# Expert layer: each slot tile split after its last block, all four multiplied as split pairs into banks 4 to 7, and h added bank by bank

## What is computed

```python
def hier_moe(xn, w_group, b_group, w_expert, b_expert, w_gate, w_up, w_down):
    ...
    cw = jnp.einsum('tk,tke->te', comb, jax.nn.one_hot(expert_id, N_EXPERTS, ...))
    hid = jax.nn.silu(jnp.einsum('td,edf->tef', xt, w_gate)) * jnp.einsum('td,edf->tef', xt, w_up)
    y = jnp.einsum('tef,efd->td', hid * cw[:, :, None], w_down)
    return y.reshape(b, s, d)
...
        h = h + hier_moe(rms_norm_2(h, ln_ffn[i]), ...)
        gate = jax.nn.sigmoid(rms_norm_2(h, ln_ple[i]) @ ple_w_gate[i])
        h = h + (gate * (p[i] @ ple_w_proj[i])).astype(h.dtype)
```

## Time and profile before

| | us |
|---|---|
| median of 3 executions | 1210.54 |
| lowest, highest | 1205.42, 1211.98 |
| the profiled execution, its own time | 1211.84 |
| its span, first to last instruction | 1210.1 |
| TensorE busy | 1090.7 (90%) |
| VectorE busy | 763.8 (63%) |
| ScalarE busy | 720.8 (60%) |
| mean granted TensorE clock | 0.946 of full speed |

### The profile page before, as it was taken

The page is one execution under the profiler, slowest core; times in us unless marked ns, Lnnn a source line. Parts: engine busy times, 40 slices in busy tenths (PEclk is TensorE's granted clock), DMA queues, the critical chain, the costliest instruction groups (busy, mean ns, idle before and its releaser), DMA issues.

```text
span 1210.1 us, 17394 instructions
## 1 busy us (share of the span) xinstructions
PE 1090.7 (90%) x6140; PEld 905.5 (75%) x6140; DVE 763.8 (63%) x1331; ACT 720.8 (60%) x1228; POOL 72.2 (6%) x111
## 2 busy tenths in 40 slices
PE   5968889999999997899979999978979969999988
PEld 4857677999998785797667777747868767787756
DVE  4536664666665665456567778765755467778864
ACT  4435664444443544385649888835656549988834
POOL 9000600000000012000100000000000100000000
PEclk9987699999999999899989999998989979999998
DMA  9784003665654545002507999853601607999830
GB/s 291 182 206 151 1 10 126 212 191 177 191 187 147 178 139 186 2 2 87 209 25 255 327 322 329 308 169 112 191 15 36 261 3 258 338 328 335 305 138 35
DMA packets 105083, 210.79 MB, mean 174 GB/s; under 512 B 7992, under 2 KB 49816, under 8 KB 104752
## 3 DMA queue, kind: packets, MB, share of 16 engines
q1 hardware_dynamic: 101984, 204.04, 49.4%
q0 software_dynamic: 2736, 4.80, 2.2%
q10 hardware_dynamic: 288, 0.99, 0.2%
HBM read 207.17 MB, written 2.62 MB: 173 GB/s over the span
## 4 chain that ended last, share of the span: by engine, by line
PE 79%; DVE 8%; ACT 5%; issue 3%; DMA 3%; SPq 1%; DVEq 1%; ACTq 0%
PE bank L794 22%; PE bank L1501 13%; PE bank L1518 9%; PE bank L1186 8%; PE bank L1196 7%; PE bank L889 4%; PE bank L870 2%; PE bank L713 2%; PE bank L878 2%; DMA expert_w<-in_moe_w_up 1%; PE bank L869 1%; PE bank L1995 1%; PE bank L1342 1%; ACT x_high L767 1%; DMA ring<-in_w_uq 1%
## 5 line engine op out<-in xcount | busy, mean ns | idle before, releaser
L794 PE MATMUL bank<-weight_parts,x_high 128*128 128x512 f32 (+3 forms) x832 | 252.1, 389 | 27.9 <-issue 15.5
L794 PEld LDWEIGHTS bank<-weight_parts,x_high 128*128 128x128 f32 x832 | 159.6, 199 | 59.1 <-issue 21.9
L1501 PE MATMUL bank<-expert_high,block_high 128*128 128x256 f32 x560 | 183.7, 328 | 2.5 <-issue 2.4
L815 DVE TENSOR_TENSOR weight_parts<-ring,weight_parts 128x1024 fp32r<-128x1024 f32 (+3 forms) x108 | 121.1, 1140 | 93.7 <-ACT weight_parts L812 93.6
L812 ACT CAST weight_parts<-ring 128x1024 fp32r<-128x1024 f32 (+3 forms) x108 | 103.8, 983 | 122.0 <-PE bank L794 95.1
L1438 DVE TENSOR_TENSOR expert_low<-expert_w,expert_high 128x1024 fp32r<-128x1024 f32 x140 | 164.9, 1218 | 11.7 <-ACT expert_high L1431 11.5
L794 PE MATMUL bank<-weight_parts,x_low 128*128 128x512 f32 (+3 forms) x416 | 160.2, 385 | 0.0
L1501 PE MATMUL bank<-expert_low,block_high 128*128 128x256 f32 x560 | 158.5, 283 | 0.0
L1501 PE MATMUL bank<-expert_high,block_low 128*128 128x256 f32 x560 | 158.5, 283 | 0.0
L1431 ACT CAST expert_high<-expert_w 128x1024 fp32r<-128x1024 f32 x140 | 140.2, 1054 | 14.3 <-DMA expert_w<-in_moe_w_up 13.9
L1518 PE MATMUL bank<-expert_w,junk 128*128 128x512 f32 x280 | 132.1, 595 | 2.6 <-DVE arena L1574 1.4
(11 more groups left out here) (330 smaller groups left out, 1732.2 us busy)
## 6 DMA issues: line engine op xcount, KB each, us to landing
expert_w<-in_moe_w_gate SPq DMA_DIRECT2D x70, 512.0 KB, 5.6
expert_w<-in_moe_w_up SPq DMA_DIRECT2D x70, 512.0 KB, 7.1
expert_w<-in_moe_w_down SPq DMA_DIRECT2D x70, 512.0 KB, 5.4
ring<-in_w_ff SPq DMA_DIRECT2D x64, 512.0 KB, 3.9
ring<-in_w_in SPq DMA_DIRECT2D x16, 512.0 KB, 11.6
ring<-in_a_w_in SPq DMA_DIRECT2D x16, 512.0 KB, 4.8
ring<-in_ple_w_gate SPq DMA_DIRECT2D x16, 512.0 KB, 5.5
ring<-in_w_o SPq DMA_DIRECT2D x8, 512.0 KB, 6.3
```

The costliest lines, as they stand in the source:

```text
L794: mm = nc.tensor.matmul(bank[:, j["m"] % 4, 0:n], j["operand"][x][:, 2 * c + kk, at[0]:at[1]], weight_parts[:, number % PAIRS, w, kk * n:( ...
L815: nc.vector.tensor_tensor(low, raw_weights, high, ALU.subtract).then_inc(weights_split, 1)
L1501: mm = nc.tensor.matmul(bank[:, 4 + b % 2, 0:256].rearrange("p (q n) -> p q n", q=2), x[:, b % 2, k, :], w[:, k], start=k == 0 and n == 0, ...
```

## The change

1. **Order on VectorE and ScalarE.** Tile 0 gets its last addition with block 31, tiles 1, 2 and 3 with blocks 32, 33 and 34. Each tile is now rounded (`round_acc(q)`, waits for `ex_added` of block 31 + q) and split (`split_acc(q)`) after its own last block. For that, `add(31)` and `split_acc(0)` stand ahead of `hid(34)`, and `round_acc(0)` ahead of the last silu.
2. **Tile 0 as a pair.** `pe_combine` has no plain float32 matmuls left: 32 fp32r matmuls in place of 4 plain ones (8 records) and 24.
3. **Upper banks.** It writes banks 4 to 7 in place of 0 to 3, and waits only for `acc_split` of each tile, no longer for all 35 blocks.
4. **Bank by bank.** The last matmul of each bank signals (`combined`), and each of the four additions to `h` waits for its own bank.

```diff
+        def round_acc(q):
+            act.wait_ge(ex_added, first + EXPERTS + q)
+            nc.scalar.copy(acc_high[:, q, :], acc[:, q * D_MODEL:(q + 1) * D_MODEL]).then_inc(acc_rounded, 1)
...
                 copy_x(b + 2)
+            if b == BLOCKS - 2:
+                round_acc(0)
         keep(BLOCKS - 1)
         for q in range(1, SORT_TILES):
-            if q == 1:
-                act.wait_ge(ex_added, first + BLOCKS)
-            nc.scalar.copy(acc_high[:, q, :], acc[:, q * D_MODEL:(q + 1) * D_MODEL]).then_inc(acc_rounded, 1)
+            round_acc(q)
...
-        pe.wait_ge(ex_added, BLOCKS * (layer + 1))
-        for t in range(TILES):
-            for half in range(2):
-                nc.tensor.matmul(bank[:, 2 * t + half, :], place_turned[:, 0, t * P:(t + 1) * P].bitcast(F32),
-                                 acc[:, half * 512:(half + 1) * 512], start=True, stop=False)
-        for q in range(1, SORT_TILES):
-            pe.wait_ge(acc_split, (SORT_TILES - 1) * layer + q)
+        for q in range(SORT_TILES):
+            pe.wait_ge(acc_split, SORT_TILES * layer + q + 1)
             for t in range(TILES):
                 for half in range(2):
                     for x in (acc_high, acc_low):
-                        mm = nc.tensor.matmul(bank[:, 2 * t + half, :], place_turned[:, q, t * P:(t + 1) * P],
-                                              x[:, q, half * 512:(half + 1) * 512], start=False,
+                        mm = nc.tensor.matmul(bank[:, 4 + 2 * t + half, :], place_turned[:, q, t * P:(t + 1) * P],
+                                              x[:, q, half * 512:(half + 1) * 512], start=q == 0 and x is acc_high,
                                               stop=q == SORT_TILES - 1 and x is acc_low)
-        mm.then_inc(down_made, 1)
+                    if q == SORT_TILES - 1:
+                        mm.then_inc(combined, 1)
...
         for b in range(BLOCKS):
             hid(b)
-            if b >= 3:
+            if 3 <= b < BLOCKS - 1:
                 add(b - 3)
+            if b == BLOCKS - 1:
+                add(BLOCKS - 3)
             if b + 2 < BLOCKS:
                 dve_split_expert(dve, layer, b + 2)
-        for b in range(BLOCKS - 3, BLOCKS):
-            add(b)
-        for q in range(1, SORT_TILES):
-            dve.wait_ge(acc_rounded, (SORT_TILES - 1) * layer + q)
-            v.tensor_tensor(acc_low[:, q, :], acc[:, q * D_MODEL:(q + 1) * D_MODEL], acc_high[:, q, :],
-                            ALU.subtract).then_inc(acc_split, 1)
-        dve.wait_ge(down_made, OPEN + UNITS + layer + 1)
+            if b == BLOCKS - 2:
+                add(BLOCKS - 4)
+                split_acc(0)
+        add(BLOCKS - 2)
+        split_acc(1)
+        add(BLOCKS - 1)
+        split_acc(2)
+        split_acc(3)
         for t in range(TILES):
             for half in range(2):
+                dve.wait_ge(combined, 4 * layer + 2 * t + half + 1)
                 cols = h[:, t, half * 512:(half + 1) * 512]
-                v.tensor_tensor(cols, cols, bank[:, 2 * t + half, :], ALU.add).then_inc(units_added, 1)
+                v.tensor_tensor(cols, cols, bank[:, 4 + 2 * t + half, :], ALU.add).then_inc(units_added, 1)
```

More of the change, by code:

```diff
@@ L342, in build_program @@
         sem(n) for n in ("ex_up", "ex_silu", "ex_hid", "ex_turned", "ex_kept", "ex_down", "ex_added"))
-    acc_rounded, acc_split = sem("acc_rounded"), sem("acc_split")
+    acc_rounded, acc_split, combined = sem("acc_rounded"), sem("acc_split"), sem("combined")
     hid_made, bent, hid_scaled, hid_high, hid_ready, down_made, units_added = (
@@ L1559, in hid, with split_acc @@
             v.tensor_tensor(hids[:, b % 2, :], silus[:, b % 2, :], bank[:, 4 + b % 2, P:2 * P], ALU.mult).then_inc(ex_hid, 1)
+        def split_acc(q):
+            dve.wait_ge(acc_rounded, SORT_TILES * layer + q + 1)
+            v.tensor_tensor(acc_low[:, q, :], acc[:, q * D_MODEL:(q + 1) * D_MODEL], acc_high[:, q, :],
+                            ALU.subtract).then_inc(acc_split, 1)
         def add(b):
```

## The result

The changed kernel takes 1200.78 us (median of 6 executions, 1198.68 to 1204.76) where the kernel before took 1210.74 us in the same comparison (6 executions, 1205.42 to 1211.98): a ratio of 0.9925, 95% interval 0.9903 to 0.9947. A second comparison later, with 6 executions of the changed kernel (median 1203.99 us) and 11 of the kernel before (1212.76 us), gave 0.993 (0.9902 to 0.9958). The forecast was 1200.5 us, with 8 in 10 between 1195.5 and 1206; both medians lie in that range. The profiled execution has a span of 1200.7 us, against 1210.1.

A forecast was written before the change was run, and what follows sets the result against it. TensorE, busy for 90% of the span, sets the pace, with idle and dear work at the combine. Two layers at 4.6 us (9.2) plus 0.9 for the clock, from the median 1210.54, give 1200.5 us; 8 in 10 between 1195.5 and 1206.

The forecast's parts named there:

- The combine: From the last down products to complete h: h complete 4.6 us earlier in each layer (4.4 to 4.8), 9.2 in all.
- TensorE's early start: Combine begins straight after the last down product, at 797.8 instead of 799.63 in layer 0: gain 1.8 us.
- The two small terms that were too careful: Combine: 0.1 us for the change of type; additions to h, spaced 0.60 to 0.73 us, finishing at a middle value, 806.9.
- The slack of the last hid: hid(34), delayed by add(31) and the split of tile 0, still precedes its transpose with 0.35 us to spare; costs nothing.
- The splits kept up: Splits of tiles 1, 2 and 3 finish before TensorE's combine wants them, with slacks of 1.0, 0.4 and 1.0 us.
- 5.5 us from h to the gate: VectorE runs without a pause after the combine, so the gate starts 5.5 us after h and earlier h arrives whole.
- The clock, 0.9 us: Gate matmuls: a shorter idle stretch before the transposes leaves layer 0's kind of loss, not layer 1's; gain 0.9 us.
- A: Rival: clock stays high into the gate, giving up to another 3.4 us: 1197, down to 1195; chance 0.12.
- B: Rival: splits or additions around the combine come late, each microsecond over a slack costing one: 1203.5 to 1205; 0.10 with E.
- D: Rival: slower, the low clock spreads through the attention of layer 1: 1217 or more; chance 0.02.
- C: Rival: some 8 us more low clock after layer 0 takes the gain away, no measurable change: 1205 to 1209; chance 0.12.
- E: Rival: something unseen holds the combine behind add(34) as before, leaving 3.2 us a layer: 1204; 0.10 together with B.

The follow-up runs named there:

- the added subtraction: The changed kernel with one more unused 128x1024 subtraction on VectorE between the split of tile 0 and hid(34): 1204.42 us, ratio 0.9934.
- the three subtractions: The changed kernel with three more unused 128x1024 subtractions on VectorE between the split of tile 0 and hid(34): 1211.55 us, ratio 0.9996.
- one signal: The changed kernel, but all four additions to h wait until the last bank is complete: 1204.05 us, ratio 0.9942.
- the pair alone: The kernel before with only tile 0 made a split pair, after all 35 blocks are added, banks 0 to 3: 1219.0 us, ratio 1.0057.
- early splits: The changed kernel with VectorE's two low parts of gate weights moved ahead of the additions to h: 1200.35 us, ratio 0.9904.

## Why the prediction was right, and where it was not

- **The combine.** Forecast 4.6 us for each layer, measured 4.89. TensorE's early start: 1.8 forecast, and 1.8 by the two traces: the combine follows the down products 5.27 us after low(32) has begun (791.03 to 796.30, where eight records of 0.43 us from 792.86 end) in place of 7.08; without it 2.26 are lost in layer 1. Tile 0 as a pair: 1.56 and 1.56. Bank by bank: 1.2 forecast (2.5 us from the last matmul to the complete `h` before, 1.3 after), measured 1.40. Taken out one at a time the three cost 5.2 us, a little more than all together; most of the excess is that of the run without the upper banks, whose combine begins later than that of the kernel before.
- **The two small terms that were too careful.** The additions to `h` keep 0.60 us between them with a wait before each: the value by the Trainium skill's rule ("VectorE: DVE Perf Modes", "The DRAIN you can't avoid", which measured a signal behind each operation; here a wait stands before each as well), not the 0.73 of the dependent pair, and not the middle that I took. A wait whose signal has come costs nothing that shows; the row of the dependent pair measured a wait for its neighbour's own end. And the 0.1 us for the change from float32 to pairs isn't there: the last matmul of the combine begins at 803.55, which is 796.30 plus 31 times 0.234. Together these are the 0.3 us between 4.6 and 4.89.
- **The slack of the last hid.** Forecast 0.35, measured 0.37 by the added subtraction. The splits kept up: TensorE's 32 matmuls have no gap, and tile 2, the tightest with 0.4 forecast, is split 0.5 us before it is wanted.
- **5.5 us from h to the gate, unchanged.** Right. But the reason in the first part, that VectorE's run without a pause sets it, was only half of it: with VectorE relieved of 2.3 us of work the gate came 0.4 us sooner after `h` and no more.
- **The clock, 0.9 us.** The number came out (29.20 against 30.13 in layer 1), the reason did not. I had said that the larger loss, 2.6 us, belongs to the longer idle stretch before the transposes and would be gone. The second execution of the changed kernel refutes it: in its layer 0 the gate takes 24.75 us, a loss of 2.7, with an idle stretch of 1.17 us before the transposes; in its layer 1 it takes 22.06, no loss at all. TensorE's timeline of that execution, the gate's first matmuls in layer 0 and in layer 1, each after 3.40 us of idle:

```profile
813.83 1.19 PE L794 MATMUL bank<-weight_parts,x_high 128*128 128x512 f32 x2 [3.40 <-issue]
...
1176.26 0.70 PE L794 MATMUL bank<-weight_parts,x_high 128*128 128x512 f32 x2 [3.40 <-issue]
```

  1.19 us for two matmuls is the low clock, 0.70 the high one. Over the 22 gates of all unfilled profiles the time is 22.05 to 22.06 in two, 23.5 to 23.7 in thirteen and 24.6 to 24.8 in seven. So the loss at the gate has one of three sizes, what decides which is not shown, and the mean of about 1.8 us a gate is what a forecast should carry on both sides; my term should have been zero, with a range. The forecast of 1200.5 would have been 1201.3, as good. What the shorter first stretch did change is the transposes themselves: behind 2.57 us of idle the clock was low in them in 4 of 8 cases (3.1 to 3.5 us for the 16, where 2.05 is usual), behind 1.17 or 1.51 us in none of 18. That bought nothing, since the gate starts 5.5 to 5.6 us after `h` either way.
- **The total.** That 1200.5 and 1200.78 agree to 0.3 us is luck: the second comparison has 1203.99. What the traces bear out is the 9.2 us of the two combines, measured 9.8, beside a spread of several microseconds in stretches that the change doesn't touch.
- **The rivals.** A (the clock gives back) came at one of the changed kernel's four profiled gates, and a larger loss at another, so it is not a gain to count on. B (a late tail) did not come: no slack was exceeded. But its price was too low: beyond the slack each microsecond costs one, and behind the 2.8 and 3.1 us of idle that the three subtractions made, TensorE's clock took 1.7 more in each layer, which brought the kernel to 0.9996. That is the way in which this change could have gone wrong, and the slower rival should have been built on it instead of on the attention (D), where the stretch from `h` to the experts of layer 1 was 181.6 us before, 181.6 and 183.5 after. C (the clock takes it all away) did not come in either comparison. E did not come; the parts taken out singly show that each did what it says.

## What to carry to other kernels

Count an idle stretch of TensorE twice: its own length, and what slow matmuls behind it may cost, here nothing in some cases and up to 2.8 us in others. That can make an early start worth more than its length, and it made the cheaper form of tile 0 alone, which gains nothing by itself (1.0018 with the idle stretch filled), a loss (1.0057); taking both together was the gain. Before an instruction is queued ahead of another engine's input, work out the slack of that input and move work only within it; here 0.37 us separated free from one for one. Where a stretch of idle can't be removed, matmuls whose result is overwritten can hold the clock: about 1.6 us for each gate, and the lowest median of this study (0.9887).

## What the runs showed of the hardware

- TensorE's granted clock fell to 1.2 GHz behind idle stretches of 1.99 us (one of two, lower banks), 2.0 us (both, before the gate in layer 0 with one signal and with the pair alone), 2.57 us (4 of 8, before the transposes), 2.8 and 3.1 us (both, three subtractions), 2.96 us (both, early splits), 3.4 us (14 of 16, before the gate) and 3.8 us (both, pair alone). It did not fall behind 1.17, 1.38 and 1.51 us (20 cases), nor at the four filled gates. At the two gates that are left (kernel before and one signal, layer 1) it was still low from the transposes. The same stretch in two layers of one execution, or in two executions, can have different outcomes.
- VectorE reading one PSUM bank is not slowed by TensorE writing the others: four additions of 128x512 take 2.48 us with and without it.
- A wait for a signal that has come costs VectorE nothing that shows: 0.60 us between additions either way. Two operations of that shape of which the second waits for the first are 0.73 us apart, 0.13 more. `add(31)`, which waits for `add(30)`, begins 0.22 us after its end, with `add`'s register work in that stretch too.
